# Thirty-two unused bytes behind each row of the normalised input, of the memory and of the weight ring

## What is computed

```python
x = x + 0.5 * swiglu(rms_norm(x, norm_ffn1_w), ffn1_w_in, ffn1_w_out)      # width 2816
x = x + hybrid_mixer(rms_norm(x, norm_mix_w), ...)   # state-space scan beside differential attention
x = x + memory_cross_attention(rms_norm(x, norm_cross_w), rms_norm(mem, norm_mem_w), ...)  # 256 rows
x = x + 0.5 * swiglu(rms_norm(x, norm_ffn2_w), ffn2_w_in, ffn2_w_out)
x = rms_norm(x, norm_final_w)
# second block: stick-breaking attention, gated convolution, then an MLP with relu squared
x = x + rms_norm_2(mixed, g_post_mix)
x = x + rms_norm_2(square(relu(rms_norm_2(x, g_pre_mlp) @ w_up)) @ w_down, g_post_mlp)
x = x + sigmoid(rms_norm_2(x, g_ple) @ w_ple_gate) * (p @ w_ple_proj)
```

## Time and profile before

| | |
|---|---|
| median of three runs | 2337.28 us |
| the profiled execution | 2337.46 us |
| its span, first to last instruction | 2335.7 us |
| TensorE busy (matmuls) | 2231.6 us, 96% |
| weight loads busy | 1788.4 us, 77% |
| VectorE, ScalarE, GpSimd busy | 867.2, 779.0, 907.4 us |
| mean granted TensorE clock | 0.988 |

### The profile page before, as it was taken

One profiled execution on the slowest core, in us unless ns is written; L12 is line 12 of the kernel. 1 busy time (PEld: TensorE's weight loads), 2 busy tenths in 40 slices (PEclk: granted clock), 3 DMA queues, 4 the chain that ended last, 5 costly groups with the idle time before them and its releaser, 6 DMA issues.

```text
span 2335.7 us, 28029 instructions
## 1 busy us (share of the span) xinstructions
PE 2231.6 (96%) x10020; PEld 1788.4 (77%) x10020; DVE 867.2 (37%) x1461; ACT 779.0 (33%) x1176; POOL 907.4 (39%) x384
## 2 busy tenths in 40 slices
PE   7999999999898988999999999999999979999998
PEld 6888888778786667867888888888845868888876
DVE  4222114847713556034222222143143457213226
ACT  4222223235324434323322233223464233212223
POOL 4444444442232104723444444444400444444444
PEclk9999999999999989999999999999999999999999
DMA  4332332231222112512333333333300313333331
GB/s 169 99 98 90 107 101 90 83 97 55 64 81 63 55 37 74 161 54 66 97 91 98 99 99 108 91 99 90 99 9 10 95 49 106 101 100 98 99 108 46
DMA packets 57873, 200.77 MB, mean 86 GB/s; under 512 B 6288, under 2 KB 7696, under 8 KB 57792
## 3 DMA queue, kind: packets, MB, share of 16 engines
q1 hardware_dynamic: 53568, 192.96, 27.2%
q10 hardware_dynamic: 4224, 6.68, 0.9%
HBM read 197.50 MB, written 2.12 MB: 85 GB/s over the span
## 4 chain that ended last, share of the span: by engine, by line
PE 55%; issue 30%; POOL 12%; DVE 3%; ACT 0%; POOLq 0%; DVEq 0%; ACTq 0%
PE bank L408 16%; PE bank L410 16%; PE bank L409 16%; POOL w_lo L374 12%; PE bank L811 2%; PE bank L830 1%; PE bank L832 1%; DVE pn_t L1833 1%; DVE gx_lo L1355 1%; PE bank L842 1%; PE bank L780 1%; DVE x L1835 1%; PE bank L470 0%; PE bank L472 0%; PE bank L471 0%
## 5 line engine op out<-in xcount | busy, mean ns | idle before, releaser
L374 POOL TENSOR_TENSOR w_lo<-w_raw,w_hi 128x1024 fp32r<-128x1024 f32 x364 | 882.4, 2426 | 1377.6 <-ACT w_hi L929 1377.3
L408 PE MATMUL bank<-gx_hi,w_hi 128*128 128x512 f32 x1696 | 669.2, 395 | 35.8 <-DVE gx_lo L1355 14.2
L410 PE MATMUL bank<-gx_hi,w_lo 128*128 128x512 f32 x1696 | 662.8, 391 | 0.0
L409 PE MATMUL bank<-gx_lo,w_hi 128*128 128x512 f32 x1696 | 662.7, 391 | 0.0
L929 ACT CAST w_hi<-w_raw 128x1024 fp32r<-128x1024 f32 x364 | 379.3, 1044 | 367.5 <-PE bank L410 326.3
L408 PEld LDWEIGHTS bank<-gx_hi,w_hi 128*128 128x128 f32 x1696 | 320.1, 189 | 111.9 <-issue 29.2
L410 PEld LDWEIGHTS bank<-gx_hi,w_lo 128*128 128x128 f32 x1696 | 319.9, 189 | 67.7
L409 PEld LDWEIGHTS bank<-gx_lo,w_hi 128*128 128x128 f32 x1696 | 320.2, 189 | 65.2
L408 PE MATMUL bank<-ff_hi,w_hi 128*128 128x512 f32 x352 | 136.9, 389 | 0.0
L409 PE MATMUL bank<-ff_lo,w_hi 128*128 128x512 f32 x352 | 136.9, 389 | 0.0
L410 PE MATMUL bank<-ff_hi,w_lo 128*128 128x512 f32 x352 | 136.9, 389 | 0.0
(11 more groups left out here) (322 smaller groups left out, 2765.9 us busy)
## 6 DMA issues: line engine op xcount, KB each, us to landing
w_raw<-wstream SPq DMA_DIRECT2D x364, 512.0 KB, 3.5
x<-xT ACTq DMA_DIRECT2D x2, 1024.0 KB, 10.4
outT<-ple_o SPq DMA_DIRECT2D x8, 256.0 KB, 2.0
square<-bias_rows ACTq DMA_DIRECT2D x4, 256.0 KB, 3.2
rfin_row<-bias_rows ACTq DMA_DIRECT2D x4, 256.0 KB, 3.1
m_T<-memT ACTq DMA_DIRECT2D x1, 1024.0 KB, 5.1
p_T<-pT ACTq DMA_DIRECT2D x1, 512.0 KB, 3.9
consts<-consts ACTq DMA_DIRECT2D x1, 448.0 KB, 11.7
```

What stands on the lines that cost most here:

```text
L374: nc.gpsimd.tensor_tensor(w_lo[:, s, :], w_raw[:, s, :], w_hi[:, s, :].bitcast(F32), ALU.subtract).then_inc(unit_lo, 1)
L408: nc.tensor.matmul(dst, hi, rhs[0], start=first, stop=False)
L409: nc.tensor.matmul(dst, hi, rhs[1], start=False, stop=False)
L410: return nc.tensor.matmul(dst, lo, rhs[0], start=False, stop=last)
```

## The change

Each chunk of gx_hi and gx_lo, each chunk of m_hi and m_lo, and each slot of w_hi and w_lo gets 8 float32 (32 bytes) behind it that nobody reads or writes. All uses are narrowed to the used columns. `w_raw` is as before, and so are all other stage buffers. To make room, wdt, the small columns and m_lo move. Chunk k of gx then begins 32k bytes further modulo 128 than chunk 0, and slot s of the ring 32s bytes further than slot 0.

```diff
+PAD = 8
-        wdt = fixed("wdt", [8, 16])
         wdt_hi = fixed("wdt_hi", [8, 16], F32R)
+        wdt_lo = fixed("wdt_lo", [8, 16], F32R)
         cursor[0] = -(-cursor[0] // LINE) * LINE
-        GX_HI, GX_LO = cursor[0], cursor[0] + DC * S * 4
-        gx_hi = fixed("gx_hi", [DC, S], F32R)
-        gx_lo = fixed("gx_lo", [DC, S], F32R)
+        GX_HI, GX_LO = cursor[0], cursor[0] + DC * (S + PAD) * 4
+        gx_hi = fixed("gx_hi", [DC, S + PAD], F32R)
+        gx_lo = fixed("gx_lo", [DC, S + PAD], F32R)
         w_raw = fixed("w_raw", [RING, UNIT])
-        w_hi = fixed("w_hi", [RING, UNIT], F32R)
-        w_lo = fixed("w_lo", [RING, UNIT], F32R)
+        w_hi = fixed("w_hi", [RING, UNIT + PAD], F32R)
+        w_lo = fixed("w_lo", [RING, UNIT + PAD], F32R)
...
-                return buf[:, c, :]
+                return buf[:, c, 0:min(buf.shape[2], S)]
...
+        wdt = at("wdt", 40, [8, 16])
...
-        m_hi = at("m_hi", 24, [DC, ML], F32R)
-        m_lo = at("m_lo", 32, [DC, ML], F32R)
+        m_hi = at("m_hi", 24, [DC, ML + PAD], F32R)
+        m_lo = at("m_lo", 84, [DC, ML + PAD], F32R)
...
-                nc.gpsimd.tensor_tensor(w_lo[:, s, :], w_raw[:, s, :], w_hi[:, s, :].bitcast(F32),
+                nc.gpsimd.tensor_tensor(w_lo[:, s, 0:UNIT], w_raw[:, s, :], w_hi[:, s, 0:UNIT].bitcast(F32),
...
-            gx = lambda k: (gx_hi[:, k, :], gx_lo[:, k, :])
+            gx = lambda k: (gx_hi[:, k, 0:S], gx_lo[:, k, 0:S])
...
-                nc.scalar.copy(w_hi[:, j, :], w_raw[:, j, :]).then_inc(unit_hi, 1)
+                nc.scalar.copy(w_hi[:, j, 0:UNIT], w_raw[:, j, :]).then_inc(unit_hi, 1)
```

More of the change, by code:

```diff
@@ L152, in build @@
         rfin_row = fixed("rfin_row", [S])
[L153 to L157, removed]
         xrec = fixed("xrec", [16])
-        y_sq, y_root, y_rstd = xmin, xsum, xrec
         REGION = -(-cursor[0] // 512) * 512
@@ L163, in build @@
         root_col = fixed("root_col", [2 * TT])
-        eps_col = fixed("eps_col", [1])
-        subln = fixed("subln", [1])
-        fin = fixed("fin", [32])
+        m_rstd = fixed("m_rstd", [MT])
+        fin = nc.alloc_sbuf_tensor_at("fin", [P, 32], F32, offset=cursor[0])
+        xmin = fixed("xmin", [16])
+        xsum = fixed("xsum", [16])
+        m_root = nc.alloc_sbuf_tensor_at("m_root", [P, MT], F32, offset=cursor[0])
+        eps_col = nc.alloc_sbuf_tensor_at("eps_col", [P, 1], F32, offset=cursor[0] + 32)
+        subln = nc.alloc_sbuf_tensor_at("subln", [P, 1], F32, offset=cursor[0] + 64)
+        cursor[0] += 96
+        y_sq, y_root, y_rstd = xmin, xsum, xrec
         REGION_END = nc.sbuf_usable_end if not callable(nc.sbuf_usable_end) else nc.sbuf_usable_end()
@@ L183, in tile_of @@
             if isinstance(c, int):
-                return buf[:, c, :]
+                return buf[:, c, 0:min(buf.shape[2], S)]
             n = buf.shape[2]
-            return buf[:, :, :].rearrange("p a b -> p (a b)")[:, ds(c * n, n)]
+            return buf[:, :, :].rearrange("p a b -> p (a b)")[:, ds(c * n, min(n, S))]
         def col(name, i):
@@ L533, in _ @@
             for k in range(DC):
-                nc.tensor.matmul(bank[6][0:SH, :], wdt_hi[:, k, :], gx_hi[:, k, :], start=(k == 0), stop=False)
-                nc.tensor.matmul(bank[6][0:SH, :], wdt_hi[:, k, :], gx_lo[:, k, :], start=False, stop=False)
-                mm = nc.tensor.matmul(bank[6][0:SH, :], wdt_lo[:, k, :], gx_hi[:, k, :], start=False,
+                nc.tensor.matmul(bank[6][0:SH, :], wdt_hi[:, k, :], gx_hi[:, k, 0:S], start=(k == 0), stop=False)
+                nc.tensor.matmul(bank[6][0:SH, :], wdt_hi[:, k, :], gx_lo[:, k, 0:S], start=False, stop=False)
+                mm = nc.tensor.matmul(bank[6][0:SH, :], wdt_lo[:, k, :], gx_hi[:, k, 0:S], start=False,
                                       stop=(k == DC - 1))
@@ L747, in m_rows @@
                 mm.then_inc(sem("m_rowed"), 1)
-            tiles("ck", lambda k: (m_hi[:, k, :], m_lo[:, k, :]), DC, 4, peel=1, n=ML,
+            tiles("ck", lambda k: (m_hi[:, k, 0:ML], m_lo[:, k, 0:ML]), DC, 4, peel=1, n=ML,
                   ready=lambda k: pe.wait_ge(sem("m_lo"), k + 1),
@@ L1042, in _ @@
                 nc.scalar.activation(square[:, :], x[:, m, :], ACT.Square).then_inc(sem("squared"), 1)
-                nc.scalar.activation(gx_hi[:, m, :], x[:, m, :], ACT.Copy, scale=col("norm_ffn1_w", m))\
+                nc.scalar.activation(gx_hi[:, m, 0:S], x[:, m, :], ACT.Copy, scale=col("norm_ffn1_w", m))\
                   .then_inc(sem("gx_hi_done"), 1)
@@ L1171, in memory_tile @@
                 nc.scalar.activation(m_sq[:, :], m_T[:, m, :], ACT.Square).then_inc(sem("m_square"), 1)
-                nc.scalar.activation(m_hi[:, m, :], m_T[:, m, :], ACT.Copy, scale=col("norm_mem_w", m))\
+                nc.scalar.activation(m_hi[:, m, 0:ML], m_T[:, m, :], ACT.Copy, scale=col("norm_mem_w", m))\
                   .then_inc(sem("m_hi"), 1)
@@ L1262, in post @@
                     act.wait_ge(sem(f"{name}_x"), m + 1)
-                    nc.scalar.activation(gx_hi[:, m, :], x[:, m, :], ACT.Copy, scale=col(weight, m))\
+                    nc.scalar.activation(gx_hi[:, m, 0:S], x[:, m, :], ACT.Copy, scale=col(weight, m))\
                       .then_inc(sem("gx_hi_done"), 1)
@@ L1676, in memory_tile @@
                 dve.wait_ge(sem("m_hi"), m + 1)
-                nc.vector.scalar_tensor_tensor(out=m_lo[:, m, :], in0=m_T[:, m, :], scalar=col("norm_mem_w", m),
-                                               in1=m_hi[:, m, :].bitcast(F32), op0=ALU.mult, op1=ALU.subtract)\
+                nc.vector.scalar_tensor_tensor(out=m_lo[:, m, 0:ML], in0=m_T[:, m, :], scalar=col("norm_mem_w", m),
+                                               in1=m_hi[:, m, 0:ML].bitcast(F32), op0=ALU.mult, op1=ALU.subtract)\
                   .then_inc(sem("m_lo"), 1)
```

## The result

The changed kernel takes 2377.48 us, the median of four runs (2373.34 to 2382.17), against 2337.39 for the kernel before (four runs). The ratio is 1.0167, with a 95% interval from 1.0144 to 1.0190. The forecast was 2337.3 with a range from 2316 to 2370; the result lies above the range, near the costliest form of the slower rival (2381).

A forecast was written before the change was run, and what follows sets the result against it. The prediction took TensorE's rate of starting products as the bound. Its terms for TensorE, the other engines and moved tensors summed as 0 + 0 + 0, leaving 2337.3 us, range 2316 to 2370.

The forecast's parts named there:

- slower rival: TensorE: shifted streams of gx and w lose the settled interval, 5.3 ns per product, 30 us, giving 2367; chance 0.34.
- What bounds the kernel: Whole kernel: TensorE, busy 96%, sets the end by how often it starts a product, every 226.7 ns; weights keep ahead.
- I take zero: TensorE product interval: no change expected, between bounds of 11 ns less and 5.3 ns more per product.
- This gait comes from when the stream began and not from where a row lies: TensorE products after interruptions: the 232 ns interval before settling at 227 was put down to the stream's starting moment.
- if loads disturb it too: TensorE: shifted weight loads also break the settled interval, 8328 x 5.3 = 44 us, giving 2381; left outside the range.
- The faster rival: TensorE: row starts clash with loads at the same place modulo 128; spreading them saves 21 to 62 us; chance 0.20.
- DVE, ACT, POOL and the moved tensors: Shifted reads and writes on these engines, and tensors at new addresses: cost zero; DVE bounded at 0.1 us.
- The weight loads: TensorE loads of 128 columns, 0.19 us: a tenth slower stays covered; beyond that, each ns costs 8.3 us.

The follow-up runs named there:

- ring_same: Changed kernel with gx and memory rows unpadded and w_lo started 384 bytes later, at w_hi's place modulo 256: 2377.94 us, ratio 1.0175 to the kernel before.
- ring_only: Changed kernel with the padding of gx and the memory rows removed, only w_hi and w_lo padded: 2380.25 us, ratio 1.0173 to the kernel before.
- lo256: Changed kernel with all padding removed and w_lo as a whole begun 256 bytes later: 2340.33 us, ratio 1.0001 to the kernel before.
- micro1: Model replaced by 49 timed blocks of 60 bare float32r products, stream and load places varied: 13.9 us per settled block, 14.0 to 14.4 otherwise.

## Why the prediction was wrong

- *What bounds the kernel* was right: the time is the number of products times their interval. 5.3 ns per product, read as the distance between the two gaits in the earlier trace rows, stands against 5.6 ns measured in ff and up and 4.8 in gx.
- *The failed step is "I take zero" for TensorE.* The term stood at 0 and measured 40.4 us, because stream and load no longer began at one place modulo 256 bytes. I took the zero from the nearest row, the flip product of the earlier trace rows. That row is plain fp32, whose columns take two beats, and isolated: it is a duration and says nothing on the interval to the next product. It should have carried no weight; then the ends 0 and +5.3 ns stood side by side, and the range had to hold the whole of the upper one. The even interval of the earlier trace rows over changing slots and chunks spoke for no effect only in appearance: all those places agreed modulo 256.
- *"This gait comes from when the stream began and not from where a row lies"* was half of it. In the kernel before, the moment decides how long settling takes. Whether there is anything to settle into is decided by the places of stream and load, as ring_same shows slot by slot. All rows of the kernel before agreed modulo 256, so its trace could not show this.
- *The slower rival had the mechanism and the price of each product, but put its bulk on the wrong set.* It gave 30 us to the shifted streams and left "if loads disturb it too", 44 us or 2381, outside the range. ring_only and ffn1_out's 2.78 us show the loads count fully. 8328 x 5.3 = 44 was the sum to use; 40 was measured.
- *The faster rival* (a clash of equal places) is reversed: equal places are the best case for 512 columns. For 256 columns it points the right way, since equal places are among the slowest there (120.0 ns against 113.3 at 64 bytes), but ck gained only 0.6 us.
- *DVE, ACT, POOL and the moved tensors* at zero were right: medians moved by 0.4% at most, and the moves cost nothing in lo256. *The weight loads* were weighed only by their length. Their busy time hardly changed, 1797.7 against 1788.4 us, but the place from which they load sets the interval between products.
- Placement does not win back the 10.9 ns between 226.7 and 215.8 ns, where the prediction had set the rule of the Trainium skill ("TensorE: Matmul & The Clock Gate", section "Wait — 56ns, not 53.3ns?") beside the trace. In 97 combinations of places none came below 226.67 at 512 columns.

Not settled: why the interval has this floor, and why the difference modulo 256 and a few places 4 bytes below a multiple of 16 (28, 60, 108, 156, 188 and 252) reach it. No run here looks into how the two reads meet.

## What to carry to other kernels

Where a stream of float32r products with a fresh load each is the bound, read the start-to-start interval in the timeline and keep streamed rows of 512 columns and loaded blocks at one place modulo 256 bytes, in every buffer that meets in one stage; padding "against conflicts" can destroy an agreement that is the fast case. An interval that is exact over hundreds of products is a state of the machine that a layout may lose, so a change of addresses is not free merely because no row of the old trace shows a cost. Test it on bare products first: three such runs of under 900 us each gave the map.

## What the hardware showed that I had not expected

- The interval between 512-column float32r products is 226.67 ns or, in other layouts, anything from 228.3 to 240.0, in short repeating patterns: 232, 235 in slot 1 of ring_same's ff products, 235, 236, 229 for a = 176 with b = 0.
- The interval depends on the place of the load, though the load (0.19 us) ends before the next start.
- 504 columns take as long as 512 (226.67), and 256 columns go at 120.0 or 113.3 ns by a 64-byte difference.
- How long a fresh stream at equal places takes to settle depends on the place: in micro1, behind the first interval of about 315 ns, two intervals near 232 ns at (128, 128), four at (64, 64), six at (32, 32), up to nine at (0, 0), and about nine in z. At (0, 0) two otherwise equal blocks took six and nine.
